# Two fused transformer layers on one core: empty steps added to the attention heads, a memory-key step and a gain load moved

## The reference

```python
# first layer
mod = silu(c) @ w_ada + b_ada                        # six vectors of 2048: w_ada is 2048 x 12288
h = rmsnorm(x) * (1 + scale_m) + shift_m             # the gain is left out here
dq, dk, dv, q_lat, kv_lat, k_pe = split(h @ w_in)
o_diff = softmax(dq0 @ dk0.T) @ dv - lam * softmax(dq1 @ dk1.T) @ dv       # 8 heads, then a norm
o_mla = softmax((q_nope @ k_nope.T + q_rope @ k_rope.T) * s) @ v           # 8 heads, q and k,v from normed latents
x = x + gate_m * (concat(o_diff, o_mla) @ w_out)
x = x + gate_f * (square(relu(mod_norm(x) @ w_ff1)) @ w_ff2)
x = rmsnorm(x, g_final)
# second layer
ya = sliding-window attention (12 heads, 4 of keys), yb = forgetting attention (12 heads)
yc = attention over 256 memory rows (4 heads): mk, mv = split(rmsnorm(mem) @ w_mem_kv)
y = sum over b of sigmoid(gate_b) * ((y_b * silu(z_b)) @ w_branch_b)
out = x + y @ w_out
```

## Time and profile before

| | |
|---|---|
| median of three runs | 2192.2 us |
| the profiled execution | 2190.42 us |
| its span, first to last instruction | 2188.6 us |
| mean granted PE clock | 0.961 |
| PE busy | 2000.1 us, 91% of the span |
| DVE busy | 1313.3 us, 60% |
| ACT busy | 945.3 us, 43% |
| POOL busy | 157.9 us, 7% |
| moved by DMA | 448.82 MB, mean 205 GB/s |

### The profile page before, as it was taken

How to read it: one execution, slowest core, us unless ns; L and a number is a source line. 1 busy time by engine, 2 the same in 40 slices (tenths; PEclk the granted TensorE clock), 3 DMA queues, 4 the chain that set the end, 5 groups by cost and what they waited for, 6 DMA issues and landing times. The chain is left out here.

```text
span 2188.6 us, 24524 instructions
## 1 busy us (share of the span) xinstructions
PE 2000.1 (91%) x9240; PEld 1642.4 (75%) x9240; DVE 1313.3 (60%) x2057; ACT 945.3 (43%) x1440; POOL 157.9 (7%) x118
## 2 busy tenths in 40 slices
PE   6598897867789999999999999979999999999999
PEld 3276775546667888888888878878988877787877
DVE  3777876776796555555555555566555545545544
ACT  2453445343444344434434455445444444444433
POOL 0100000001000110110010021110100001101000
PEclk9798999878999999999999999989999999999999
DMA  9798775657797555555555555434534456656644
GB/s 356 284 327 307 244 250 199 235 189 278 290 340 255 192 192 184 192 193 186 188 193 187 187 193 179 149 100 126 164 108 149 126 169 198 192 182 187 194 170 170
DMA packets 128967, 448.82 MB, mean 205 GB/s; under 512 B 14288, under 2 KB 14544, under 8 KB 128336
## 3 DMA queue, kind: packets, MB, share of 16 engines
q1 hardware_dynamic: 124928, 433.74, 59.8%
q0 software_dynamic: 1568, 7.34, 0.9%
q10 hardware_dynamic: 2352, 6.17, 0.7%
HBM read 443.00 MB, written 4.19 MB: 204 GB/s over the span
## 5 line engine op out<-in xcount | busy, mean ns | idle before, releaser
L283 DVE TENSOR_TENSOR wlo<-raw,whi 128x1024 fp32r<-128x1024 f32 (+4 forms) x652 | 784.9, 1208 | 750.3 <-ACT whi L282 695.5
L282 ACT ACTIVATE whi<-raw 128x1024 fp32r<-128x1024 f32 (+4 forms) x652 | 658.3, 1012 | 836.6 <-PE g L397 707.0
L392 PE MATMUL g<-whi,lhsA_hi 128*128 128x512 f32 (+4 forms) x1840 | 715.8, 391 | 35.6 <-DVE lhsA_lo L788 28.0
L393 PE MATMUL g<-whi,lhsA_lo 128*128 128x512 f32 (+4 forms) x1840 | 698.0, 381 | 0.0
L397 PE MATMUL g<-wlo,lhsA_hi 128*128 128x512 f32 (+4 forms) x1840 | 470.0, 378 | 0.2 <-DVE wlo L283 0.2
L392 PEld LDWEIGHTS g<-whi,lhsA_hi 128*128 128x128 f32 x1840 | 357.3, 194 | 99.0 <-ACT tmp L780 21.8
L393 PEld LDWEIGHTS g<-whi,lhsA_lo 128*128 128x128 f32 x1840 | 357.6, 194 | 53.8 <-issue 1.4
L397 PEld LDWEIGHTS g<-wlo,lhsA_hi 128*128 128x128 f32 x1840 | 344.4, 193 | 56.2 <-DVE wlo L283 0.4
L537 DVE SCALAR_TENSOR_TENSOR raw<-raw,srow 128x1024 f32<-128x1024 f32 x181 | 217.5, 1224 | 17.8 <-DMA raw<-in_w_ada 17.5
L392 PE MATMUL g<-whi,lhsF_hi 128*128 128x512 f32 x512 | 200.6, 392 | 0.0
L393 PE MATMUL g<-whi,lhsF_lo 128*128 128x512 f32 x512 | 199.4, 389 | 0.0
(11 more groups left out here) (250 smaller groups left out, 1471.8 us busy)
## 6 DMA issues: line engine op xcount, KB each, us to landing
raw<-in_w_ff SPq DMA_DIRECT2D x256, 512.0 KB, 3.5
raw<-in_w_ada SPq DMA_DIRECT2D x181, 512.0 KB, 4.8
raw<-in_w_in SPq DMA_DIRECT2D x176, 512.0 KB, 4.2
raw<-in_w_out SPq DMA_DIRECT2D x64, 512.0 KB, 5.0
raw<-in_w_in SPq DMA_DIRECT2D x80, 384.0 KB, 3.1
raw<-in_w_branch_a SPq DMA_DIRECT2D x12, 512.0 KB, 3.5
raw<-in_w_branch_b SPq DMA_DIRECT2D x12, 512.0 KB, 4.3
raw_wide<-in_w_ada SPq DMA_DIRECT2D x11, 512.0 KB, 7.6
```

The costliest lines, as they stand in the source:

```text
L282: t_hi = AC.put(lambda e: e.activation(hi, x, ACT.Copy), landed, free, us=0.2 + n * 0.00167)
L283: t_lo = DV.put(lambda e: e.tensor_tensor(lo, x, hi.bitcast(F32), ALU.subtract), landed, t_hi, free, us=0.15 + n * 0.00208)
L392: PE.put(lambda e, o=o, x=xh, w=h, f=first: e.matmul(o, x, w, start=f, stop=False), w, mark=False, us=us)
L393: PE.put(lambda e, o=o, x=xl, w=h: e.matmul(o, x, w, start=False, stop=False), mark=False, us=us)
```

## The change

`mem_keys` is put into `bg` later, just ahead of the input's first units, and gets four empty steps. All three kinds of head get two more `yield`s: one ahead of the transposes of the probabilities, one between their copy and the product with the values. The second halves of the input units and the query units are run with `steps=2`. The load of `gfin` moves from `reload` to behind the output projection.

```diff
     def mem_keys(r, tok):
         yield from heads_norm(r, 4, 128, tok)
+        for _ in range(4):
+            yield
         for j in range(2):
...
-    bg.append(mem_keys(r, ks))
     bg.append(row_norms(xs, t_x, ssx, rx, "rx"))
...
         s.release([kt])
+        yield
         T = yield from grab(TB)
         tok = turn_rows(T, [pb.quad[:, t, P * i:P * i + P] for i in range(2) for t in range(2)], kt)
...
         T.release([k])
+        yield
         O = yield from grab(OB)
...
         if i < 4:
-            got = run(u_in[i], width=4)
+            got = run(u_in[i], steps=2, width=4)
...
-            mark(("dv", j), sum_parts(run(u_in[i], width=4), i, dv[:, :, 512 * j:512 * j + 512], fence))
+            mark(("dv", j), sum_parts(run(u_in[i], steps=2, width=4), i, dv[:, :, 512 * j:512 * j + 512], fence))
 
     def latent_units(i):
-        r, ks = row_unit(u_q[2 * i], width=4)
+        r, ks = row_unit(u_q[2 * i], steps=2, width=4)
...
+    bg.append(mem_keys(r, ks))
     for i in range(6):
         par, tok = run(u_h0[i], width=3)
...
-        t_of["gfin"] = load(PO, gfin, a["g_final"].rearrange("(a d) -> a d", a=1).to_broadcast([P, D]), w)
...
     bg.append(spread(1, [DV.tok()]))
+    t_of["gfin"] = load(PO, gfin, a["g_final"].rearrange("(a d) -> a d", a=1).to_broadcast([P, D]), fence)
```

## The result

| | before | after |
|---|---|---|
| median, us | 2191.4 | 2177.4 |
| runs, us | 6, 2189.8 to 2193.0 | 6, 2172.3 to 2184.3 |
| ratio, 95% interval | | 0.9938, 0.9919 to 0.9958 |
| profiled execution (its span), us | 2190.4 (2188.6) | 2184.3 (2182.5) |

The change is worth 14 us. I had forecast 36: the sign and the place of the first gain were right, the size was not.

The account below looks back on a forecast made before the run. The prediction took PE's in-order queue plus its waits, and the clock, to bound the kernel. Terms -10 + 2 - 2 - 9 - 4 - 2 - 12 = -37 us gave 2155 us, forecast 2135 to 2170 (0.62), range 2128 to 2188.

Parts of the forecast that it names:

- Term 1: Memory units, before the first split matmul: moving the memory keys removes PE's wait for POOL's norm, -10 us.
- that rival: First 231 us: DMA paces throughout, so the early gain is given back; 2174 us in all, chance 0.16.
- Term 2: Latent unit, 110 to 231 us: PE's wait for w_ada's modulated rows grows, +2 us, bounds 0 and +10.
- term 3: First layer's heads, 231 to 423 us: fewer transpose and tail waits against doubled steps, added w_ada parts covered; -2 us.
- Term 4: First layer, 423 to 517 us: empty steps shorten the product's wait (-5), fewer w_ada parts (-4); -9 us.
- The rival of the choked heads: First layer's heads, 231 to 423 us: doubled steps choke VectorE and ScalarE, +42 us there; 2204 in all, chance 0.12.
- Term 5: Reload of x, about 517 us: with g_final's load later, PE's wait behind x shrinks, -4 us, bounds 0 and -8.
- Term 6: 517 to 705 us: fewer w_ada parts left, against g_final's 1 MB coming in; -2 us, bounds -8 and +3.
- Term 7: Second layer's heads, 1390 to 1760 us: empty steps take 9 us of waits, better clock 3 us; -12 us.

Follow-up runs that it names:

- e7: The changed kernel, with a difference head giving the product's bank back after VectorE's copy and squares read from the copy: 2177.2 us.
- e15: The changed kernel without empty steps in the first layer's heads (steps still doubled), w_ada products cut to 128 of 1024 columns, tiles 40 to 84: 2140.1 us.
- e14: The changed kernel without its edits of the first layer's heads, w_ada products cut to 128 of 1024 columns from tile 40 to 84: 2141.8 us.
- e5: The changed kernel without the empty steps in the first layer's sixteen heads, steps still doubled: 2173.9 us.
- e3: The changed kernel without its edits of the first layer's heads (no empty steps there, single steps): 2174.4 us.
- e13: The changed kernel with the products of w_ada's parts cut to 128 of 1024 columns from tile 40 to 84: 2150.4 us.
- e17: The changed kernel without its first-layer head edits, w_ada parts given out behind the heads' steps of a gap, tiles 40 to 84: 2154.5 us.
- e18: The changed kernel without first-layer empty steps (steps doubled), w_ada parts given out behind the heads' steps, tiles 40 to 84: 2157.9 us.
- e12: The kernel before with only g_final's load moved behind the reload of x: 2187.8 us.
- e1: The kernel before with only the memory keys' step moved later and given four empty steps: 2182.8 us.

## Why the prediction was off, step by step

- **Term 1, right.** -10 forecast; the first split matmul is 10.8 us earlier, and POOL's norm is in none of the waits before 100 us. The keys alone keep 7.7 us to the end, so the early gain is not owed; that rival falls. For POOL's products beside the weights' split I had taken 0. POOL, then VectorE beside it, one instruction to a line:

```profile
162.60 1.99 POOL L733 TENSOR_TENSOR row<-row,small 128x512 f32<-128x512 f32 x1 [89.22 <-DVE small L418]
164.55 2.02 POOL L733 TENSOR_TENSOR row<-row,small 128x512 f32<-128x512 f32 x1
```

```profile
162.46 1.23 DVE L283 TENSOR_TENSOR wlo<-raw,whi 128x1024 fp32r<-128x1024 f32 x1
163.60 2.07 DVE L283 TENSOR_TENSOR wlo<-raw,whi 128x1024 fp32r<-128x1024 f32 x1
165.59 2.06 DVE L283 TENSOR_TENSOR wlo<-raw,whi 128x1024 fp32r<-128x1024 f32 x1
```

  Two of VectorE's three splits took some 0.84 us longer than the first, 1.7 us in all. The Trainium skill ("SBUF — State Buffer", section "SBUF: two separate sides") states that of a VectorE instruction with two SBUF inputs and a GpSimd instruction that reads SBUF the one that starts first gets the shared ports for its whole length, and the other waits. The trace agrees: the records of the two engines overlap, but they end in turn, 0.9 to 1.1 us apart (163.69, 164.59, 165.67, 166.57, 167.65). The loss of 0.83 us for each was right, and it met two splits, not up to four.
- **Term 2, right in kind.** A wait of 12 to 14 us was forecast and 13.9 stands there; the stage from tile 0 to 40 grew by 4 us, not 2. The three waits that I read from the earlier trace rows were two, since the first is that of the earlier trace rows; the longest, on which the term rests, is right.
- **Terms 3 and 4: the step that failed is term 3.** Together they were to give 11 us, and the changed kernel stands 3 us behind the one without these edits. Term 4 came out near its size: tiles 76 to 88 took 86.0 us instead of 93.5, where -9 was forecast, though not for its first reason: the product's 6.7 us there became 6.0 for its bank, and part of the heads' work had moved ahead (PE has 248 instructions in that stage instead of 269). Term 3 was to be -2, but tiles 40 to 76 took 209.1 us instead of 191.8 (204.6 in e7). Two of its prices were too low.

  The first is +2 for two steps in one gap, with "the added steps take two thirds of the 6.7 away". From tile 40 to 88 they took away all of the product's wait for the copy, 11.0 us before; but the product then met its bank still in use, and the scores theirs. These two waits went from nothing to 10.0 us and from 7.4 to 16.6, so PE's wait moved by one bank. Giving the bank back earlier (e7) moved it once more and gained nothing. Even without most of the parts' work doubling lengthens tiles 40 to 76 by 8 us (183.2 in e15, 175.1 in e14).

  The second is "Covered, I say", which put the 18 us of the additional parts at nothing. With the parts' work in place the same doubling lengthens those tiles by 16 us (e5 against e3), so by these four single executions I estimate that about 8 us of the parts' work were not covered there, although over the whole run doubling alone costs nothing (2173.9 against 2174.4). I had compared VectorE's busy time with the stage's length and found 52 us free. That sum says nothing of who stands in front of whom. All parts of the stage cost 27 to 34 us in any of the three orders (e13 to e15), although VectorE is idle for nearly a quarter of it; 16 to 20 of these us go when a part of 1.2 us no longer sits ahead of the maximum, the scaling or the copy that PE waits for (e17, e18).

  The rival of the choked heads had this sign: the third stage grew and its clock fell, from 0.93 to 0.89. But its price of 42 us was far too high, and its condition (over 222 us for that stage) was not met.
- **Term 5, wrong.** 4 us were forecast at PE's wait behind x. It went from 7.6 to 6.9 us, and with g_final alone moved it stays at 7.7. x did not wait for g_final. In the changed kernel x even landed 2.7 us later. Why stays open: in both kernels, and in e12, seven loads of SP start between 8 us before and 12 us behind its issue.
- **Term 6.** -2 forecast; tiles 88 to 140 took 185.7 instead of 188.3 us.
- **Term 7, half right.** -12 forecast; the stage from tile 380 to 524 is 6.9 us shorter (449.0 to 442.1; e1 and e12, with the old second layer, have 446.1 and 446.2, so the 449.0 may read 3 us long), and the steps of the second layer alone give 5.9. Of the 6.9 us 4.8 are waits, where 9 were forecast, and 2.0 are PE's busy time at a clock of 0.97 instead of 0.96, where 3 were. The three waits of the products went as said, 9.5 us; but the waits that were not POOL's came to 10.6 us instead of about 6, since L1436's wait for VectorE grew from 1.4 to 6.1 us and one of 2.7 us is new.

Measured against the forecast of -36: 11 to 14 us are missing in the first layer's heads, 6 in the second layer, up to 4 at the reload.

What stays open: why one empty step alone costs 15 to 17 us in the first layer and two together 3, why x landed later, and what the 4 us of e12 are.

## What to carry to other kernels

Free time on an engine is no cover: before costing added work there at nothing, look in its queue at what the work stands in front of, and whether another engine waits for that. Where background work fills an engine's gaps, give it out behind the step that the critical chain needs, not ahead of it; here that exchange was worth more than every move of the chain's own steps. A wait that ends at a shared buffer moves to the next buffer when its chain is spread out, so count who else uses the buffers that the later step takes.

## What the runs showed of the hardware

- 2 MB of x took 11.2 us from issue to landing with 1 MB of g_final right behind it, and 11.3 us without it (e12): the second transfer cost the first nothing that can be seen. In the changed kernel, also without it, x took 13.9 us.
- At 162 us of the changed kernel VectorE and POOL took turns: beside POOL's two products VectorE's splits took 2.07 and 2.06 us instead of 1.23, and the instructions of the two engines ended in turn, 0.9 to 1.1 us apart.
- A stage's time can fall by 17 us with more work on its busiest helper: VectorE was busy for 219 of 285 us in e3 and for 225 of 265 in e17, with PE's granted clock at 0.90 and 0.92 (tiles 40 to 88 take 284.7 and 267.4 us).
